# Attention pairs among the projections: values, scores and turns in one group instead of two

## The chip, the cores and the metric

One core of one Trainium2 chip runs the whole kernel. The metric is the device time of one execution in microseconds; the median of three runs of the kernel before is 2280.51 us (2280.38 to 2281.26). Five engines work side by side and meet only at semaphores: PE (TensorE, matrix multiplies), DVE (VectorE), ACT (ScalarE), POOL (GpSimd) and SP (which here issues DMAs). Each runs its own instructions in the order in which they are written. A `wait_ge` stops everything behind it on that engine.

## The reference, cut to what matters

A trunk of two layers over 512 tokens of width 1024, in float32. Each layer is a gated feed-forward net, a token mixing of three branches, and a second feed-forward net. The change touches the first branch, attention, and the projections that run beside it:

```
z = h @ w_in[i]                       # h: 512 x 1024, one combined projection
q, k, v = z[..., 0:768], z[..., 768:1536], z[..., 1536:2304]   # 3 groups x 4 heads x 64
y_a = dilated_attention_mixture(q, k, v)
gates = sigmoid(z[..., G_OFF:] + b_gate[i])
merged = gates[0] * (y_a @ w_proj_a) + gates[1] * (y_b @ w_proj_b) + gates[2] * (y_c @ w_proj_c)
# attention of one group: s = q k^T / 8, masked to a dilated causal window;
# p = exp(s - max); o = (p @ v) / sum(p); the groups are mixed by their softmax denominators
```

## The kernel before, in words

Activations are kept transposed: channels on the 128 partitions, the 512 tokens along the free axis. Each float32 product is made of three passes over rounded parts (high x high, high x low, low x high), so a projection of 128 output channels is 8 x 3 = 24 matmuls of 512 columns, called a half here. A unit of weights is 1024 x 256, two halves. SP loads it into one of two raw buffers, ACT copies it rounded (`split` on ACT, L985), and DVE makes the rest (`split` on DVE, L1465). Then TensorE may use it, and the raw buffer is free for SP's next load.

The attention is worked in eight pairs (two heads, one residue of the token index modulo 4) per layer. The three dilation groups are one softmax over 640 keys, since mixing by denominators is the same as one common denominator. A pair needs:

- scores (`score_pair`, L869 and L877): matmuls in 64 x 64 tiles of the array, into `side[0]` for one head and `psum[1]` for the other, columns 0 to 639;
- on DVE the masked row maximum of each head (`score_max`, L2001) into `p_tile`, on ACT the exponential with its sum (`exponential`, L1367), on DVE the division (`normalise`, L2024 and L2025);
- turns (`turn_pair`, L889 and L894): five transposes of 128 columns for each head, the first head's into `side[1]`, the second's into `side[0]`, columns 0 to 639;
- on ACT the copies of the turned tiles into `pT` (`take_turned`, L1372 and L1374);
- values (`value_pair`, L909): 24 matmuls of 64 wide tiles into `side[1]`, columns 640 to 767;
- the head's output, copied rounded by ACT (`head_hi`, L1353), with the rest by DVE (`head_lo`, L1994), which then raises `head_made`.

All this stands between projection matmuls. `project_to(end)` (L852) issues projection matmuls up to number `end` of the 288 of the phase (twelve halves, for the remaining queries and keys and the first gates), all into `psum[0]`, whose two column halves alternate. A half may begin only when DVE has taken the half before the last (`take_half`, L1971, L1975, L2043, which raises `evacuated[0]`). Two lists written out by hand, `SCORES_AT` and `TURNS_AT`, say before which projection matmul each pair's work comes. At `SCORES_AT[n]` the scores of pair n are issued and behind them the values of pair n - 1; at `TURNS_AT[n]` the turns of pair n. So the projections are interrupted sixteen times in a layer; the values of the last pair follow the phase.

ACT and DVE have loops over the same eight pairs, with weight splits, halves and, on ACT for pairs 5 and 6, the gates' sigmoids (`sigmoids`, L1360) put in at fixed places. Sigmoid and exponential need different tables on ACT, and a table load stands at each switch. In ACT's loop the order for pair n is: head of pair n - 1, a split for n = 1 and 5, two exponentials, a split for n = 2, 3 and 6, the two copies of the turned tiles, the sigmoids.

`side` and `psum` tensors are 1024 columns wide, two banks of 512 columns each.

Of the kernel before, what the change touches and what calls it, by code (L numbers as in the profile page):

```python
# [23 lines left out]
ACT = mybir.ActivationFunctionType  # L24

P = 128
# [49 lines left out]
def trunk(nc, x, ffn1_norm, ffn1_w_gate, ffn1_w_up, ffn1_w_down, mix_norm, w_in, b_gate, b_ln_g,  # L76
# [16 lines left out]
    ATT = HEADS * RES  # L93
    PAIRS = ATT // 2
# [4 lines left out]
    KEYS = NEAR + 2 * P  # L99
# [23 lines left out]
    with ExitStack() as ctx:  # L123
# [196 lines left out]


        PHASE = 6 * 2 * 3 * KD
        SCORES_AT = (10, 48, 86, 124, 162, 194, 226, 258)
        TURNS_AT = (38, 76, 114, 152, 185, 217, 249, 281)
        MASK_STEPS = 1 + P // RES + (RES - 1) + 6 * RES


# [219 lines left out]
        def _(pe):  # L547
# [10 lines left out]
            def begin_side(s):  # L558
                pe.wait_ge(side_evacuated[s], counts[f"sv{s}"].next())
                return side[s]  # L560
# [179 lines left out]
            for layer in range(DEPTH):  # L740
# [100 lines left out]
                def project_to(end):  # L841

                    for q in range(stream["at"], end):
                        h, k, n = q // (3 * KD), q // 3 % KD, q % 3
                        c = h % 2
                        if q % (3 * KD) == 0:
                            pe.wait_ge(evacuated[0], free + max(h - 1, 0))
                            if c == 0:
                                stream["w"] = unit()
                        whi, wlo = stream["w"]  # L850
                        l, r = ((whi, h_hi), (whi, h_lo), (wlo, h_hi))[n]
                        mm = nc.tensor.matmul(psum[0][:, c * S:(c + 1) * S], l[:, k * UNIT_N + c * P:k * UNIT_N + (c + 1) * P],  # L852
                                              r[:, k * S:(k + 1) * S], start=(k == 0 and n == 0), stop=(k == KD - 1 and n == 2))
                        if k == KD - 1 and n == 2:
                            mm.then_inc(half_done if c == 0 else unit_done, 1)
                    stream["at"] = end
# [26 lines left out]
                def turn_pair(n):  # L883
                    pe.wait_ge(p_made, counts["p"].next())
                    if n == 0:

                        pe.wait_ge(side_evacuated[1], counts["sv1"].now(1))
                    for c in range(KEYS // P):
                        mm = nc.tensor.transpose(side[1][:, c * P:(c + 1) * P], p_tile[0][:, c * P:(c + 1) * P], ident[:, :])  # L889
                    mm.then_inc(pT_written, 1)  # L890
                    pe.wait_ge(p_made, counts["p"].next())
                    o = begin_side(0)
                    for c in range(KEYS // P):
                        mm = nc.tensor.transpose(o[:, c * P:(c + 1) * P], p_tile[1][:, c * P:(c + 1) * P], ident[:, :])  # L894
                    mm.then_inc(pT_written, 1)

                def value_pair(n):
                    jp, r = divmod(n, RES)

                    pe.wait_ge(pT_made, counts["pT"].next())  # L900
                    pe.wait_ge(side_evacuated[0], counts["sv0"].now(1 if n == PAIRS - 1 else 0))
                    pe.wait_ge(head_made, counts["head"].next())

                    parts = ((0, 1, P, 0, P), (0, 2, 2 * P, 0, P), (0, 0, 0, 0, HQ), (0, 3, HQ, HQ, P),
                             (1, r, NEAR, 0, P), (2, r, NEAR + P, 0, P))
                    for m, (g, t, c0, q0, q1) in enumerate(parts):
                        for b in range(2):
                            col = t * A_WIDTH + g * A_OUT + (2 * jp + b) * HEAD_DIM
                            mm = nc.tensor.matmul(side[1][rows_of(b), KEYS + q0:KEYS + q1], v[:, col:col + HEAD_DIM],  # L909
                                                  pT[b][:, c0:c0 + q1 - q0], start=(m == 0), stop=(m == len(parts) - 1))  # L910
                            if m == len(parts) - 1:
                                mm.then_inc(head_done, 1)

                for n in range(PAIRS):
                    project_to(SCORES_AT[n])
                    score_pair(n)
                    if n > 0:
                        value_pair(n - 1)
                    project_to(TURNS_AT[n])
                    turn_pair(n)  # L920
                project_to(PHASE)
                value_pair(PAIRS - 1)

                def project(last_head=False):
                    columns(begin(1), unit(), yb_hi, yb_lo, range(KB), True, True).then_inc(unit_done, 1)
# [46 lines left out]
        def _(act):  # L972
# [68 lines left out]
            def step(k=UNIT_K, n=UNIT_N, parts=1, home=None, before=0):  # L1041

                split(k, n, parts, home, before)
                counts["unit"].next()
# [201 lines left out]
            for layer in range(DEPTH):  # L1246
# [96 lines left out]
                counts["ev1"].next()  # L1343

                counts["sd0"].next(PAIRS)
                counts["se0"].next(ATT)
                counts["sd1"].next()

                def head_hi(n):
                    jp, r = divmod(n, RES)  # L1350
                    act.wait_ge(head_done, counts["head"].next(2))
                    dst = ya_hi[:, jp * S:(jp + 1) * S].rearrange("p (i r) -> p r i", r=RES)[:, r, :]
                    nc.scalar.activation(dst, side[1][:, KEYS:KEYS + P], ACT.Copy).then_inc(ya_hi_made, 1)  # L1353
# [14 lines left out]
                                         accum_out=row_sum[:, b:b + 1]).then_inc(exp_made, 1)  # L1368

                def take_turned():  # L1370
                    act.wait_ge(pT_written, counts["pT_written"].next())
                    nc.scalar.activation(pT[0][:, :], side[1][:, 0:KEYS], ACT.Copy).then_inc(pT_made, 1)  # L1372
                    act.wait_ge(pT_written, counts["pT_written"].next())
                    nc.scalar.activation(pT[1][:, :], side[0][:, 0:KEYS], ACT.Copy).then_inc(side_evacuated[0], 1)  # L1374

                bias_col = T_BGATE + layer * (3 * KD)
                counts["ev0"].next(6)
# [1 line left out]
                for n in range(PAIRS):  # L1379
                    if n == 0:  # L1380
                        step(parts=2)
                    if n > 0:
                        head_hi(n - 1)
                    if n == 1:
                        step(parts=2)
                    if n == 5:
                        step()
                    for b in range(2):
                        exponential(b)
                    if n in (2, 3):  # L1390
                        step()
                    if n == 6:
                        step(KB)
                    take_turned()
                    if n in (5, 6):

                        counts["ev0"].next()
                        sigmoids(n - 5, 0, bias_col)
                head_hi(PAIRS - 1)
                counts["ev0"].next()  # L1400

# [39 lines left out]
        def _(dve):  # L1441
            counts = {k: Count() for k in ("unit", "hi", "step", "h_hi", "sq", "acc", "side0", "side1", "std", "rstd",
                                           "silu", "act_hi", "gelu", "ln_std", "yc_hi", "yb_hi", "exp",
                                           "head", "gate", "merged", "pooled", "y", "half", "scored_b", "unit7",
                                           "l0", "l1", "l2", "s_hi", "t", "acc_hi", "pool_hi")}
            counts |= {k: Count(1) for k in ("ev0", "ev1", "se0", "se1")}
            slot = [0]

# [377 lines left out]
            for layer in range(DEPTH):  # L1826
# [181 lines left out]

                def score_max(n):
                    dve.wait_ge(side_done[0], counts["side0"].next())  # L2010
                    nc.vector.memset(small[:, 126:127], 0.0)
                    v_ = side_out(0, masked_max(n, 0, side[0]))
                    dve.wait_ge(side_evacuated[0], v_)
                    negate(0)
                    counts["se0"].next()
                    dve.wait_ge(scored_b, counts["scored_b"].next())
                    nc.vector.memset(small[:, 126:127], 0.0)
                    v_ = evac(1, masked_max(n, 1, psum[1]))
                    dve.wait_ge(evacuated[1], v_)
                    negate(1)  # L2020
# [23 lines left out]
                                                        rstd[:, :], ALU.mult))  # L2044

                for n in range(PAIRS):
                    score_max(n)
                    if n > 0:
                        head_lo(n - 1)
                    normalise(0)  # L2050
                    normalise(1)
                    if n < 4:
                        take_half((0, 2, 3, 5)[n])
                        split()
                        if n in (0, 2):
                            take_half((1, None, 4)[n])
                    elif n in (4, 7):
                        take_half(6 if n == 4 else 10)
                        take_half(7 if n == 4 else 11)
                    elif n == 5:  # L2060
                        split()
                        take_half(8)
                    else:
                        take_half(9)
                        split(KB)
                head_lo(PAIRS - 1)

                def project(d):
# [69 lines left out]
```

## Time and profile before

| | us |
|---|---|
| median of 3 runs | 2280.51 |
| the profiled execution | 2280.67 |
| its span | 2278.9 |
| TensorE busy | 2269.5 (100%) |
| DVE busy | 1535.8 (67%) |
| ACT busy | 854.7 (38%) |
| POOL busy | 31.0 (1%) |
| DMA, mean over the span | 98 GB/s |

The granted clock of TensorE is at full speed (2.4 GHz) in all 40 slices of the span. Busy time of TensorE is that of pipelined matmuls, whose ends overlap the starts of the next, so the time from start to start tells more than the length. The phase of the change lies at 499.6 to 596.0 us in the first layer and at 1627.2 to 1723.6 us in the second. The profiled execution took 1.8 us more than its span, and 0.16 us more than the median.

### The profile page before, as it was taken

The page shows a single profiled execution, that of the slowest core. Times are in us where ns is not written, and L with a number is a line of the kernel's source. Part 1 is how long each engine was busy: PE and PEld are TensorE (multiplying, and loading weights), DVE is VectorE, ACT ScalarE, POOL GpSimd, SP SyncE. Part 2 cuts the span into 40 slices and gives each one's busy share as a digit, 9 for nine tenths or more (in the row PEclk, how much of TensorE's full clock was granted, in tenths as well). Part 3 has the DMA queues.
Part 4 walks back from the last instruction along what each step waited for, and adds up shares of the span by engine and source line. Part 5 has one row for each costly group of instructions (what it writes and reads, how often), then busy time and mean ns, then how long its engine had stood idle before and what let it go on. Part 6 is the DMA issues. An engine that isn't in the chain of part 4 may idle for free.

```text
span 2278.9 us, 31164 instructions
## 1 busy us (share of the span) xinstructions
PE 2269.5 (100%) x13365; PEld 1988.8 (87%) x13365; DVE 1535.8 (67%) x1728; ACT 854.7 (38%) x936; POOL 31.0 (1%) x70
## 2 busy tenths in 40 slices
PE   9999999999999999999999999999999999999998
PEld 8898998888888888989888989888888888899897
DVE  6895977545543668959568959675554455698694
ACT  5443433323522334424334424342344224344342
POOL 5000000000000000000000000000000000000000
PEclk9999999999999999999999999999999999999999
DMA  5324233321223332323323333342212332233231
GB/s 163 97 93 129 75 111 116 93 78 61 79 83 100 117 97 88 112 93 112 103 89 104 99 106 97 107 134 65 83 52 83 102 115 94 79 109 128 76 114 70
DMA packets 231393, 222.66 MB, mean 98 GB/s; under 512 B 4209, under 2 KB 229601, under 8 KB 231265
## 3 DMA queue, kind: packets, MB, share of 16 engines
q1 hardware_dynamic: 225744, 215.29, 29.9%
q10 hardware_dynamic: 5520, 5.51, 0.7%
q8 instruction: 99, 1.62, 0.3%
q14 instruction: 30, 0.24, 0.0%
HBM read 218.69 MB, written 2.10 MB: 97 GB/s over the span
## 4 chain that ended last, share of the span: by engine, by line
PE 100%; DVE 0%; POOL 0%; DVEq 0%; issue 0%; ACT 0%; POOLq 0%
PE psum L584 56%; PE psum L632 16%; PE side L632 12%; PE psum L852 6%; PE psum L786 2%; PE side L584 1%; PE psum L596 1%; PE side L909 1%; PE side L869 1%; PE psum L734 0%; PE side L889 0%; PE side L894 0%; PE side L797 0%; PE side L877 0%; PE side L766 0%; PE psum L708 0%
## 5 line engine op out<-in xcount | busy, mean ns | idle before, releaser
L584 PE MATMUL psum<-h_hi,w_hi 128*128 128x512 f32 x928 | 361.9, 390 | 0.0
L584 PE MATMUL psum<-h_hi,w_lo 128*128 128x512 f32 x928 | 361.1, 389 | 0.0
L584 PE MATMUL psum<-h_lo,w_hi 128*128 128x512 f32 x928 | 361.0, 389 | 0.0
L1465 DVE TENSOR_TENSOR w_lo<-raw,w_hi 128x2048 fp32r<-128x2048 f32 (+2 forms) x123 | 239.2, 1945 | 80.7 <-ACT w_hi L985 80.0
L632 PE MATMUL psum<-s_hi,hi 128*128 128x256 f32 x1024 | 289.8, 283 | 0.0
L632 PE MATMUL psum<-s_lo,hi 128*128 128x256 f32 x1024 | 289.8, 283 | 0.0
L985 ACT ACTIVATE w_hi<-raw 128x2048 fp32r<-128x2048 f32 (+2 forms) x123 | 200.9, 1633 | 228.9 <-PE psum L584 198.7
L584 PE MATMUL psum<-act_hi,w_lo 128*128 128x512 f32 x704 | 273.9, 389 | 0.0
L1094 ACT ACTIVATE hi<-t_sum 128x1536 fp32r<-128x1536 f32 (+1 forms) x128 | 134.2, 1055 | 264.7 <-DVE t_sum L1660 264.7
L584 PE MATMUL psum<-act_hi,w_hi 128*128 128x512 f32 x576 | 224.1, 389 | 0.0
L584 PE MATMUL psum<-act_lo,w_hi 128*128 128x512 f32 x576 | 224.1, 389 | 0.0
L632 PE MATMUL psum<-s_hi,t_lo 128*128 128x256 f32 x768 | 217.3, 283 | 0.0
L632 PE MATMUL side<-s_lo,hi 128*128 128x256 f32 x768 | 217.3, 283 | 0.0
L632 PE MATMUL side<-s_hi,hi 128*128 128x256 f32 x768 | 217.3, 283 | 0.0
L584 PEld LDWEIGHTS psum<-h_hi,w_lo 128*128 128x128 f32 x928 | 174.2, 188 | 36.3
L584 PEld LDWEIGHTS psum<-h_hi,w_hi 128*128 128x128 f32 x928 | 174.2, 188 | 36.0
L584 PEld LDWEIGHTS psum<-h_lo,w_hi 128*128 128x128 f32 x928 | 174.2, 188 | 35.9
L632 PEld LDWEIGHTS psum<-s_hi,hi 128*128 128x128 f32 x1024 | 196.6, 192 | 0.0
L632 PEld LDWEIGHTS psum<-s_lo,hi 128*128 128x128 f32 x1024 | 196.6, 192 | 0.0
L1532 DVE SCALAR_TENSOR_TENSOR xT<-psum,xT 128x1024 f32<-128x1024 f32 x53 | 64.8, 1224 | 139.6 <-PE psum L584 139.3
L584 PEld LDWEIGHTS psum<-act_hi,w_lo 128*128 128x128 f32 x704 | 132.1, 188 | 27.4
L632 PEld LDWEIGHTS side<-s_hi,hi 128*128 128x128 f32 x768 | 147.4, 192 | 0.3
(285 smaller groups left out, 4318.0 us busy)
## 6 DMA issues: line engine op xcount, KB each, us to landing
raw<-in_ffn_w_up_dram SPq DMA_DIRECT2D x44, 1024.0 KB, 5.4
raw<-in_ffn_w_gate_dram SPq DMA_DIRECT2D x43, 1024.0 KB, 5.4
raw<-in_w_in_dram SPq DMA_DIRECT2D x42, 1024.0 KB, 5.3
raw<-in_ffn_w_down_dram SPq DMA_DIRECT2D x32, 1024.0 KB, 5.0
raw<-in_ffn_w_down_dram SPq DMA_DIRECT2D x16, 768.0 KB, 4.4
raw<-in_w_in_dram SPq DMA_DIRECT2D x24, 512.0 KB, 4.1
raw<-in_w_out_dram SPq DMA_DIRECT2D x8, 1024.0 KB, 5.0
raw<-in_w_proj_b_dram SPq DMA_DIRECT2D x8, 512.0 KB, 3.4
```

The source lines that it names most:

```text
L584: mm = nc.tensor.matmul(dst[:, c * S:(c + 1) * S], l[:, a], r[:, b], start=first and k == ks[0] and n == 0, stop=last and k == ks[-1] and ...
L596: mm = nc.tensor.matmul(o, l[:, k * P:(k + 1) * P], r[:, k * S:(k + 1) * S], start=(k == 0 and n == 0), stop=(k == KD - 1 and n == 2))
L632: mm = nc.tensor.matmul(o[:, col:col + HALF], l(k), r[:, b], start=k == 0 and n == 0, stop=k == KH - 1 and n == 2)
L786: mm = nc.tensor.matmul(d, l[:, k * S + t * P:k * S + (t + 1) * P], w[:, part, k], start=(k == 0 and m == 0), stop=(k == KD - 1 and m == 2))
L852: mm = nc.tensor.matmul(psum[0][:, c * S:(c + 1) * S], l[:, k * UNIT_N + c * P:k * UNIT_N + (c + 1) * P], r[:, k * S:(k + 1) * S], start=( ...
L869: nc.tensor.matmul(outs[b][h * HQ:(h + 1) * HQ, col:col + k1 - k0], t[rows_of(b), q + h * HQ:q + (h + 1) * HQ], t[rows_of(b), k + k0:k + k ...
L909: mm = nc.tensor.matmul(side[1][rows_of(b), KEYS + q0:KEYS + q1], v[:, col:col + HEAD_DIM], pT[b][:, c0:c0 + q1 - q0], start=(m == 0), sto ...
L985: nc.scalar.activation((home[0] if home else w_hi[s])[:, 0:k * n], raw[s][:, 0:k * n], ACT.Copy).then_inc(hi_made, 1)
L1094: nc.scalar.activation(dst, src, ACT.Copy).then_inc(hi_made, 1)
L1465: nc.vector.tensor_tensor(lo[:, a], raw[s][:, a], hi[:, a].bitcast(F32), ALU.subtract).then_inc(split_made, 1)
L1532: i_ = nc.vector.scalar_tensor_tensor(x_, src, scale, x_, ALU.mult, ALU.add)
```

## The change

TensorE interrupts the projections at the places of one list. Group n holds the values of pair n - 2, the scores of pair n and the turns of pair n - 1, in this order. Groups 0 to 8 stand among the projections (0: scores alone; 1: scores and turns; 8: values and turns), the last values behind them as before. The second head's turned tiles move to columns 640 and up: three of them in `side[0]`, two in `psum[1]`; ACT copies them in two pieces, ahead of the first head's. TensorE's turns wait, from pair 1 on, for `head_made` of the values in the same group. DVE's maximum of pair n waits for the copies of the second head's turned tiles of pair n - 1. On ACT and DVE each head is worked one pair later, and ACT's copies of the turned tiles come ahead of the exponentials. In the diff TensorE's part comes first, then ACT's (from `take_turned`), then DVE's (from `score_max`).

```diff
-        SCORES_AT = (10, 48, 86, 124, 162, 194, 226, 258)
-        TURNS_AT = (38, 76, 114, 152, 185, 217, 249, 281)
+        GROUPS_AT = (10, 48, 82, 122, 162, 194, 220, 245, 270, PHASE)
+        TURNED_B = KEYS
...
                     mm.then_inc(pT_written, 1)
                     pe.wait_ge(p_made, counts["p"].next())
-                    o = begin_side(0)
                     for c in range(KEYS // P):
-                        mm = nc.tensor.transpose(o[:, c * P:(c + 1) * P], p_tile[1][:, c * P:(c + 1) * P], ident[:, :])
+                        o, at_ = (side[0], TURNED_B + c * P) if c < 3 else (psum[1], TURNED_B + (c - 3) * P)
+                        mm = nc.tensor.transpose(o[:, at_:at_ + P], p_tile[1][:, c * P:(c + 1) * P], ident[:, :])
                     mm.then_inc(pT_written, 1)
 
                 def value_pair(n):
...
-                    pe.wait_ge(pT_made, counts["pT"].next())
-                    pe.wait_ge(side_evacuated[0], counts["sv0"].now(1 if n == PAIRS - 1 else 0))
+                    pe.wait_ge(pT_made, counts["pT"].next(2))
                     pe.wait_ge(head_made, counts["head"].next())
...
-                for n in range(PAIRS):
-                    project_to(SCORES_AT[n])
-                    score_pair(n)
-                    if n > 0:
-                        value_pair(n - 1)
-                    project_to(TURNS_AT[n])
-                    turn_pair(n)
-                project_to(PHASE)
-                value_pair(PAIRS - 1)
+                for n in range(PAIRS + 2):
+                    project_to(GROUPS_AT[n])
+                    if n > 1:
+                        value_pair(n - 2)
+                    if n < PAIRS:
+                        score_pair(n)
+                    if 0 < n <= PAIRS:
+                        if n > 1:
+                            pe.wait_ge(head_made, counts["head"].now(1))
+                        turn_pair(n - 1)
...
                 def take_turned():
-                    act.wait_ge(pT_written, counts["pT_written"].next())
+                    act.wait_ge(pT_written, counts["pT_written"].next(2))
+                    nc.scalar.activation(pT[1][:, 0:3 * P], side[0][:, TURNED_B:TURNED_B + 3 * P], ACT.Copy)
+                    nc.scalar.activation(pT[1][:, 3 * P:KEYS], psum[1][:, TURNED_B:TURNED_B + 2 * P], ACT.Copy).then_inc(pT_made, 1)
                     nc.scalar.activation(pT[0][:, :], side[1][:, 0:KEYS], ACT.Copy).then_inc(pT_made, 1)
-                    act.wait_ge(pT_written, counts["pT_written"].next())
-                    nc.scalar.activation(pT[1][:, :], side[0][:, 0:KEYS], ACT.Copy).then_inc(side_evacuated[0], 1)
...
                 for n in range(PAIRS):
                     if n == 0:
                         step(parts=2)
+                    if n > 1:
+                        head_hi(n - 2)
                     if n > 0:
-                        head_hi(n - 1)
+                        take_turned()
                     if n == 1:
                         step(parts=2)
...
                     if n == 6:
                         step(KB)
-                    take_turned()
                     if n in (5, 6):
...
+                head_hi(PAIRS - 2)
+                take_turned()
                 head_hi(PAIRS - 1)
...
                 def score_max(n):
                     dve.wait_ge(side_done[0], counts["side0"].next())
+                    if n > 0:
+                        dve.wait_ge(pT_made, counts["pT"].next(2) - 1)
...
                 for n in range(PAIRS):
+                    if n > 1:
+                        head_lo(n - 2)
                     score_max(n)
-                    if n > 0:
-                        head_lo(n - 1)
                     normalise(0)
                     normalise(1)
...
-                    elif n in (4, 7):
-                        take_half(6 if n == 4 else 10)
-                        take_half(7 if n == 4 else 11)
+                    elif n == 4:
+                        take_half(6)
+                        take_half(7)
+                    elif n == 7:
+                        take_half(10)
...
+                counts["pT"].next(2)
+                head_lo(PAIRS - 2)
+                take_half(11)
                 head_lo(PAIRS - 1)
```

## Rows read from the trace of the kernel before

**Rows 1.** The page, part 1: engine, busy us (share), instructions.

```profile
PE 2269.5 (100%) x13365; PEld 1988.8 (87%) x13365; DVE 1535.8 (67%) x1728; ACT 854.7 (38%) x936; POOL 31.0 (1%) x70
```

**Rows 2.** The page, part 4: the chain that ended last, by engine.

```profile
PE 100%; DVE 0%; POOL 0%; DVEq 0%; issue 0%; ACT 0%; POOLq 0%
```

**Rows 3.** Busy time of each engine in the first layer's phase.

```profile
499.55:595.95 96.40, 96.40 (x786) 78.30 (x784) 51.74 (x122) 45.55 (x70) 0.00 (x0) 1.00 0.19 58
```

**Rows 4.** The chain of waits in order of time: start, length, what.

```profile
488.83 10.88 PE psum L596 x48
```

**Rows 5.** Timeline, TensorE, pairs 0 and 1: start, length, engine, line, operation.

```profile
501.59 0.39 PE L852 MATMUL psum<-h_hi,w_hi 128*128 128x512 f32 x1
...
509.45 0.39 PE L852 MATMUL psum<-h_lo,w_hi 128*128 128x512 f32 x1
509.69 0.71 PE L889 MATMUL side<-ident,p_tile 128*128 128x128 f32 x5
510.23 0.71 PE L894 MATMUL side<-ident,p_tile 128*128 128x128 f32 x5
510.69 0.48 PE L852 MATMUL psum<-h_hi,w_lo 128*128 128x512 f32 x1
511.01 0.39 PE L852 MATMUL psum<-h_hi,w_hi 128*128 128x512 f32 x1
...
512.85 0.39 PE L852 MATMUL psum<-h_hi,w_lo 128*128 128x512 f32 x1
513.16 0.53 PE L869 MATMUL side<-qk 64*64 64x384 f32 x1
...
514.41 1.33 PE L909 MATMUL side<-pT,v 128*64 128x128 f32 x24
515.67 0.50 PE L852 MATMUL psum<-h_hi,w_hi 128*128 128x512 f32 x1
...
521.93 0.40 PE L852 MATMUL psum<-h_hi,w_hi 128*128 128x512 f32 x1
```

**Rows 6.** Timeline at the phase's end, TensorE, ACT and DVE.

```profile
594.37 0.40 PE L852 MATMUL psum<-h_hi,w_lo 128*128 128x512 f32 x1
594.69 1.33 PE L909 MATMUL side<-pT,v 128*64 128x128 f32 x24
...
596.09 0.41 ACT L1353 ACTIVATE ya_hi<-side 128x128 fp32r<-128x128 f32 x1 [2.16 <-PE side L909]
...
596.53 0.40 DVE L1994 TENSOR_TENSOR ya_lo<-side,ya_hi 128x128 fp32r<-128x128 f32 x1 [1.04 <-ACT ya_hi L1353]
```

**Rows 7.** Forms of L852 and L909: count, then ns min/median/max.

```profile
L852 PE MATMUL psum<-h_lo,w_hi x192: 387/389/504, 499.8 to 1721.8; 128*128 128x512 f32 x192
...
L909 PE MATMUL side<-pT,v x384: 219/272/323, 514.4 to 1723.4; 128*64 128x128 f32 x128, 128*64 128x64 f32 x64
```

**Rows 8.** Timeline, ACT, pairs 5 and 6.

```profile
564.61 1.93 ACT L985 ACTIVATE w_hi<-raw 128x2048 fp32r<-128x2048 f32 x1
566.43 0.81 ACT L1367 ACTIVATE p_tile<-p_tile,small 128x640 f32<-128x640 f32 x1
...
571.69 1.28 ACT L1360 ACT_TABLE_LOAD   x1
572.99 1.33 ACT L1360 ACTIVATE gate<-gate,table 128x512 f32<-128x512 f32 x2
...
578.97 1.06 ACT L985 ACTIVATE w_hi<-raw 128x1024 fp32r<-128x1024 f32 x1
```

**Rows 9.** Timeline, DVE, pair 5.

```profile
568.85 2.29 DVE L1465 TENSOR_TENSOR w_lo<-raw,w_hi 128x2048 fp32r<-128x2048 f32 x1
571.05 0.69 DVE L2043 TENSOR_TENSOR gate<-psum,rstd 128x512 f32<-128x512 f32 x1
```

**Rows 10.** ACT's copies out of PSUM of 256 and 640 columns: ns min/median/max.

```profile
L1154 ACT ACTIVATE wide<-side x64: 361/366/370, 112.3 to 2215.5; 128x256 f32<-128x256 f32 x64
...
L1372 ACT ACTIVATE pT<-side x16: 706/706/710, 510.4 to 1720.3; 128x640 f32<-128x640 f32 x16
```

More of the change, by code:

```diff
@@ L1345, in _ @@
                 counts["sd0"].next(PAIRS)
-                counts["se0"].next(ATT)
+                counts["se0"].next(PAIRS)
                 counts["sd1"].next()
@@ L1444, in _ @@
                                            "head", "gate", "merged", "pooled", "y", "half", "scored_b", "unit7",
-                                           "l0", "l1", "l2", "s_hi", "t", "acc_hi", "pool_hi")}
+                                           "l0", "l1", "l2", "s_hi", "t", "acc_hi", "pool_hi", "pT")}
             counts |= {k: Count(1) for k in ("ev0", "ev1", "se0", "se1")}
@@ L2014, in score_max @@
                     negate(0)
-                    counts["se0"].next()
                     dve.wait_ge(scored_b, counts["scored_b"].next())
```

## The prediction

> **What bounds the kernel now.** I read the busy shares first, then the chain of waits, then the phase that the change touches, instruction by instruction. TensorE is busy for 2269.5 of 2278.9 us [rows 1], and the chain that ended last is TensorE's to 100% [rows 2]. So a change counts only by what it does to the order, the length and the gaps of TensorE's own stream. The phase (projection matmuls of L852 with the attention pairs between them) is 96.40 us of each layer at a granted clock of 1.00 [rows 3]. A run of matmuls of 512 columns goes at 10.88 / 48 = 0.2267 us each, start to start [rows 4]. The phase has 288 of them, 65.28 us; what stands between them is 31.1 us. No stretch of TensorE in it waits for another engine; its gaps are those at a change from one kind of matmul to another.
>
> **What an interruption costs now.** From the last projection matmul before it to one some steps later, less 0.2267 a step [rows 5]:
> - turns (ten transposes): 509.45 to 512.85, ten steps: 3.40 - 2.27 = 1.13 us. The transposes run at 0.54 / 5 = 0.109 us each, so 1.09 us is the work. An interruption by turns alone costs almost nothing beyond it.
> - scores alone: 501.59 to 509.45, 28 steps: 7.86 - 6.35 = 1.51.
> - scores and values: 512.85 to 521.93, 28 steps: 9.08 - 6.35 = 2.73.
> - values alone, behind the phase, up to the next matmul: 1.26 + 0.32 [rows 6].
>
> **The change on TensorE, with no wait.** Each old pair has 1.13 + 2.73 = 3.86. The new group is values, scores, turns, and I add it from blocks: entry into the values 0.32 (594.37 to 594.69 [rows 6]; about the same into the scores, 512.85 to 513.16 [rows 5]); values to next block 1.26 (514.41 to 515.67); scores to next block 1.25 (513.16 to 514.41); turns to the second matmul behind them 1.32 (509.69 to 511.01); the steps behind it are 0.03 longer in sum (511.01 to 512.85, eight steps) [rows 5]. Not shown before is a transpose that directly follows 64-wide tiles. A first projection matmul there is 504 instead of 389 ns and a first value matmul 323 instead of 272 [rows 7] (+0.115 and +0.05). The transpose (272 ns) is nearer to the value matmul in length, so I take 0.07 for it, with 0 and 0.115 as bounds. Sum 4.25, less two steps (0.45): 3.80. Six such groups save 6 x 0.06 = 0.36. The group of scores 1 and turns 0 is 0.32 + 1.25 + 1.32 + 0.10 - 0.45 = 2.54 against 2.64: saves 0.10. The group of values 6 and turns 7 is 2.55, against 2.73 - 1.51 = 1.22 for the values within the old group plus 1.13: costs 0.20. The first scores and the last values stay. Nothing is won by "one interruption for two": 0.36 + 0.10 - 0.20 = 0.26, or 0.36 if I total the phase (31.1 measured, against 1.51 + 2.54 + 22.80 + 2.55 + 1.36 = 30.76). I take 0.36 us per layer. Bounds: if the turns' first step is 0.115 dearer, 0.0; if it costs nothing, and the 0.20 gap from scores to the next block shrinks to the 0.10 between values (both halves), 1.7.
>
> The rows say why: of the old 16 breaks the eight turn breaks had no price. The Trainium skill (TensorEngine Tiling (Array Packing), Key Properties) says that a change of tiling mode drains the TensorE. By that rule turns, which use the whole array as the projections do, were free to enter and leave, and the new group has the same three changes (projection to values, to scores, to turns) as the old score group; the trace agrees, 0.24 us from projection to transpose against 0.31 from projection to scores. By that rule alone the saving would be 0 where the rows give 0.36.
>
> **What the change adds: waits on the head.** From pair 1 on, the turns wait for head_made of the values in the same group. These values have to be copied by ACT (L1353) and subtracted by DVE (L1994) first. Queued behind that wait on TensorE are the ten transposes and all projections. The clean chain is at the end of the phase [rows 6]: values 594.69 + 1.33 = 596.02, ACT 596.09 to 596.50, DVE 596.53 to 596.93: 0.91 us. For DVE to TensorE no row shows a hop; I take 0.05, like the 0.03 and 0.07 of the other two. So the turns may start 0.96 behind the end of the values.
> - Groups 2 to 5: the scores stand between. Turns would start 1.26 + 1.25 - 1.33 = 1.18 behind that end: covered with 0.22 to spare, if both engines are free. Counting on from each group's end, they are (DVE's last split ends about 0.6 us or more before the copy of the head does, the tightest being group 2).
> - Group 8 (values 6, turns 7): no scores between. The turns would start 0.07 before the values end, so TensorE waits 0.96 + 0.07 = 1.03 us. This is certain by the order alone; bounds 0.96 and 1.15.
> - Group 6: let E be the end of the turns of group 5. 26 matmuls, then values and scores: the second matmul is at E + 0.07, the 26th 5.47 later, turns due at 5.54 + 0.32 + 1.26 + 1.25 = E + 8.37. ACT copies the three parts of the turned tiles first (about 0.47, 0.37 and 0.71, overlapped by 0.1) [rows 10], to E + 1.38, then the weight split (starts E + 1.28; exponentials 1.82 later [rows 8]), then DVE's chain: 2.42 from the first exponential to its own split, that 2.29 and overlapped, gate half 8 up to 2.89 behind the split's start [rows 8, 9]. E + 1.28 + 1.82 + 2.42 + 2.89 = 8.41, head 0.30 net, hop 0.05: E + 8.76. TensorE waits 0.39. ACT's sigmoids end at about E + 7.5 and aren't last. Bounds 0 and 0.8.
> - Group 7: turns due at E + 8.14 (25 matmuls). ACT's split for the next phase needs half 9, whose last matmul ends at E + 4.57: split 4.67 to 5.74 (1.06), table load 1.28, two sigmoids 1.33 [rows 8]: E + 8.39. Only then the head's copy (0.3 net), DVE 0.42, hop: E + 9.16. TensorE waits 1.02. The sigmoids used to stand behind the turns' copies, where nothing waited; now they stand in front of the head. Bounds 0.6 and 1.4.
>
> Together 0.39 + 1.02 + 1.03 = 2.44 us per layer.
>
> **What else moves, at nothing.** DVE's row maxima now wait for the copies of the turned tiles (E + 0.8) in place of following the scores; behind them are queued exponentials, normalisations, halves and splits. Probabilities are then ready at E + 4.5 (5.6 with an ACT split before, 5.3 with a table load) and are wanted at 8.1 or later. Halves: the tightest is half 6, taken by about E + 5.2, wanted at E + 6.7. Weight splits are three us or more early, and so the DMAs of SP's queue, issued when a split frees its raw buffer, move by a us or two with a whole unit (over 10 us) of cover. The copy in three in place of two costs ACT 0.1. If the cover of a half or split were gone, each us late would be a us on TensorE.
>
> **Sum.** 2.44 - 0.36 = 2.08 per layer, 4.2 for two. The profiled execution has 2280.67, 0.16 over the median 2280.51: so 2284.7 (+0.18%). About 0.2% (4.6 us) is what a measurement can tell from no change, so this lies just inside.
>
> **Rivals.**
> - Slower: the scores don't cover the head in groups 2 to 5. It decides from 1.18 us between the end of the values and the release of TensorE. If that takes 1.40, four groups pay 0.22 and the other three 0.44 more each: +2.2 per layer, 2289.1. For: the slack is 0.22 and the last hop is on no row. Against: all hops shown are 0.03 to 0.07. Chance 0.12.
> - Slower: a switch of ACT's table stops it for twice the 1.28 us of the load. Then the wait of group 6 is 1.15 (by ACT, not DVE) and that of group 7 3.3: 1.15 + 3.3 + 1.03 - 0.36 = 5.1 per layer, 2290.7. Against: the sigmoid begins 0.02 behind the load's end [rows 8]. Chance 0.03. The Trainium skill (ScalarE: Activation LUTs, What ACT_TABLE_LOAD costs) gives a drain of about 1380 ns besides the load of 1283, by which the time would be near 2291; this trace has the load and not the drain.
> - Only group 8 waits, since ACT and DVE run ahead of my count: 1.03 - 0.36 = 0.67 per layer, 2281.8. For: two long chains added from rows. Chance 0.14.
> - Faster: breaks are dearer than counted (saving 1.7) and only group 8 waits: -1.4 to -3, 2279 or so. Against: turns alone cost 1.13 for 1.09 of work. Chance 0.05, and hardly ever beyond 0.2%.
>
> **How the numbers follow.** The forecast has 0.66, own range 2283.4 to 2285.9, and 0.20 of it lies above 2285.07. Slower by over 0.2%: 0.20 + 0.12 + 0.03 = 0.35; faster 0.03; within 0.62. The range 2281.4 to 2286.6 leaves out most of the slower rivals and the faster one.
>
> **What would show it.** Profile after: transposes of group 8 start about 1.0 us later than the values end, released by DVE's L1994-line; group 7 the same, behind sigmoids; group 6 by a few tenths, behind DVE's gate half; groups 2 to 5 without a gap; phase 98.5 us in place of 96.4; a transpose behind scores at a first step of about 0.18. It is wrong if groups 2 to 5 show gaps, if group 7 has none, or if the phase without its waits is shorter by over 1 us.

## The result, and the profile after

The changed kernel takes 2284.44 us, the median of 20 runs (2284.08 to 2285.28), against 2280.82 (20 runs, 2280.29 to 2281.52) for the kernel before on the same chips. The ratio is 1.0016, 95% interval 1.0010 to 1.0023: 3.6 us slower, 0.16%. The forecast was 2284.7, range 2281.4 to 2286.6, with the higher chance on a difference within 0.2%. In the comparisons below, two executions of the kernel before ran at a lower granted clock (0.85 and 0.556; 2480.51 and 3784.57 us) and are left out of the ratios.

The page after, parts 1 and 4, which answer to [rows 1] and [rows 2]:

```profile
PE 2268.5 (99%) x13365; PEld 1988.5 (87%) x13365; DVE 1537.8 (67%) x1728; ACT 857.1 (38%) x952; POOL 30.2 (1%) x70
...
PE 98%; ACT 1%; DVE 1%; DMA 0%; issue 0%; DVEq 0%; ACTq 0%
```

TensorE's busy time fell by 1.0 us, and the span rose. ACT and DVE now hold 1% each of a chain that was TensorE's alone: the new time is waits, not work.

The phase in both layers, busy time by engine (columns as in [rows 3]):

```profile
499.26:597.53 98.27, 96.11 (x785) 78.23 (x784) 52.57 (x122) 46.98 (x78) 0.00 (x0) 1.00 0.19 57
1628.84:1727.12 98.28, 96.12 (x785) 78.23 (x784) 52.60 (x122) 46.98 (x78) 0.00 (x0) 1.00 0.19 57
```

The phase is 1.87 and 1.88 us longer than the 96.40 of [rows 3], at the same granted clock. The two together are 3.75, and the medians differ by 3.6. Outside the phases only the time before the first one differs, by 0.29 (499.26 against 499.55); among the profiles of the experiments it lies between 499.26 and 499.76, in kernels that are alike up to there, so this is scatter between executions.

The timeline of the kernel after, TensorE, ACT and DVE, around groups 2, 6, 7 and 8 (start, length, engine, line, operation, and in brackets the idle time before it with what ended it):

```profile
521.67 0.39 PE L852 MATMUL psum<-h_hi,w_hi 128*128 128x512 f32 x1
521.99 1.33 PE L908 MATMUL side<-pT,v 128*64 128x128 f32 x24
523.25 0.53 PE L869 MATMUL side<-qk 64*64 64x384 f32 x1
...
524.50 0.77 PE L889 MATMUL side<-ident,p_tile 128*128 128x128 f32 x5
...
525.56 0.48 PE L852 MATMUL psum<-h_lo,w_hi 128*128 128x512 f32 x1
...
534.52 0.39 PE L852 MATMUL psum<-h_lo,w_hi 128*128 128x512 f32 x1
...
568.04 2.28 DVE L1468 TENSOR_TENSOR w_lo<-raw,w_hi 128x2048 fp32r<-128x2048 f32 x1
568.39 1.33 PE L908 MATMUL side<-pT,v 128*64 128x128 f32 x24
...
569.90 0.40 ACT L1353 ACTIVATE ya_hi<-side 128x128 fp32r<-128x128 f32 x1
570.25 0.68 DVE L2047 TENSOR_TENSOR gate<-psum,rstd 128x512 f32<-128x512 f32 x1
570.85 0.37 DVE L1997 TENSOR_TENSOR ya_lo<-side,ya_hi 128x128 fp32r<-128x128 f32 x1
571.27 0.77 PE L889 MATMUL side<-ident,p_tile 128*128 128x128 f32 x5 [0.31 <-DVE ya_lo L1997]
...
577.25 1.06 ACT L985 ACTIVATE w_hi<-raw 128x1024 fp32r<-128x1024 f32 x1 [0.22 <-PE psum L852]
...
578.22 1.33 PE L908 MATMUL side<-pT,v 128*64 128x128 f32 x24
578.33 1.28 ACT L1360 ACT_TABLE_LOAD   x1
579.63 1.33 ACT L1360 ACTIVATE gate<-gate,table 128x512 f32<-128x512 f32 x2
580.87 0.37 ACT L1353 ACTIVATE ya_hi<-side 128x128 fp32r<-128x128 f32 x1
581.27 0.38 DVE L1997 TENSOR_TENSOR ya_lo<-side,ya_hi 128x128 fp32r<-128x128 f32 x1 [1.70 <-ACT ya_hi L1353]
581.71 0.77 PE L889 MATMUL side<-ident,p_tile 128*128 128x128 f32 x5 [0.91 <-DVE ya_lo L1997]
...
588.65 1.33 PE L908 MATMUL side<-pT,v 128*64 128x128 f32 x24
...
590.05 0.39 ACT L1353 ACTIVATE ya_hi<-side 128x128 fp32r<-128x128 f32 x1 [2.58 <-PE side L908]
590.48 0.38 DVE L1997 TENSOR_TENSOR ya_lo<-side,ya_hi 128x128 fp32r<-128x128 f32 x1 [1.63 <-ACT ya_hi L1353]
590.91 0.77 PE L889 MATMUL side<-ident,p_tile 128*128 128x128 f32 x5 [0.94 <-DVE ya_lo L1997]
```

How to read it. In group 2 the transposes (L889) start 1.25 behind the scores, the time that the scores took before the values in the kernel before (513.16 to 514.41 [rows 5]): no wait. That no bracket stands there would not show it by itself, since a wait of 0.2 us can go without one (see the doubled low part below). In groups 6, 7 and 8 a bracket stands, and the releaser is each time DVE's low part of the head (L1997). In group 8 the head's chain is alone: the values end at 588.65 + 1.33 = 589.98, the transposes start at 590.91, 0.93 later. In group 7 ACT is in a table load and two sigmoids when the values end (579.55), and the head's copy starts at 580.87 only. In group 6 ACT does its copy with a small delay, and DVE is still in the gate half (570.25 + 0.68 = 570.93) when the copy ends at 570.30. The bracket is somewhat less than the added time, since it is counted from modelled ends. So below a wait is the start-to-start distance from the last scores or values to the first transpose, less the 0.20 that it takes without a wait.

### The profile page after: what moved, and what is told of

Read it like the earlier page. It is cut to its first block, busy times and chain, and to the rows that moved or that the text cites. A ratio compares the mean times of both kernels' runs of the same rounds, so it can differ in the third digit from the quotient of the medians.

```text
span 2282.4 us, 31192 instructions
## 1 busy us (share of the span) xinstructions
PE 2268.5 (99%) x13365; PEld 1988.5 (87%) x13365; DVE 1537.8 (67%) x1728; ACT 857.1 (38%) x952; POOL 30.2 (1%) x70
## 4 chain that ended last, share of the span: by engine, by line
PE 98%; ACT 1%; DVE 1%; DMA 0%; issue 0%; DVEq 0%; ACTq 0%
PE psum L584 56%; PE psum L632 16%; PE side L632 12%; PE psum L852 5%; PE psum L786 2%; PE side L584 1%; PE psum L596 1%; PE side L908 1%; PE side L889 1%; PE psum L734 0%; PE side L869 0%; PE side L797 0%; DMA x_in<-in_x_dram 0%; ACT w_hi L985 0%; PE side L766 0%; PE side L808 0%
```

## Experiments

The phase's length is given for the first layer; the second differs by 0.02 us or less. Each of the first four was compared with the kernel before at 2280.88 (33 runs), the last four at 2280.68 (29 runs), on one chip each. "Less than after" is a difference to 2284.44, which was measured with another set; the medians of the kernel before differ by 0.2 us between the sets.

**Turns before the values in group 8.** TensorE turns pair 7 before the values of pair 6, so that it needs only the head of pair 5:

```
+    if n == PAIRS:                       # TensorE
+        pe.wait_ge(head_made, counts["head"].now(1))
+        pe.wait_ge(pT_made, counts["pT"].now(2))
+        turn_pair(n - 1)
...
+    act.wait_ge(head_made, (layer + 1) * PAIRS)   # ACT, before its last copies
```

> In group 8 alone the turns of pair 7 are issued ahead of the values of pair 6, so that they wait for no head of their own group; ACT's copy of those turned tiles waits until the head of pair 6 is done. Theory (three waits of TensorE for a head: 0.38, 0.98 and 1.01 us in groups 6, 7 and 8 of each layer): the 1.01 goes, and going from transposes to values and from values to projections costs about 0.17 more than before, so -0.84 per layer: -1.7 against the changed kernel, +1.9 against the kernel before. Rival (the wait only moves on, to the last values, whose tiles are now copied later): no change against the changed kernel, +3.6 against the kernel before.

Measured: 2282.59 (11 runs, 2282.18 to 2283.21), ratio 1.0007 [0.9998, 1.0016]; 1.85 less than after. The timeline of this kernel, TensorE, group 8:

```profile
588.43 0.40 PE L852 MATMUL psum<-h_hi,w_lo 128*128 128x512 f32 x1
588.66 0.71 PE L889 MATMUL side<-ident,p_tile 128*128 128x128 f32 x5
589.21 0.49 PE L894 MATMUL side<-ident,p_tile 128*128 128x128 f32 x3
...
589.85 1.33 PE L908 MATMUL side<-pT,v 128*64 128x128 f32 x24
591.10 0.50 PE L852 MATMUL psum<-h_hi,w_hi 128*128 128x512 f32 x1
...
595.09 0.39 PE L852 MATMUL psum<-h_hi,w_lo 128*128 128x512 f32 x1
```

The transposes of group 8 start 0.23 behind the projection, as in the kernel before, the waits of groups 6 and 7 stay (0.38 and 0.99), and the phase is 97.32, 0.95 less. The wait has not moved on to the last values, which start 0.32 behind the last projection (595.09 to 595.41). So this wait is the order's alone, and half of the loss is this one place. The phase gives back 0.06 less than the 1.01 of the wait: group 8 by itself costs 595.09 - 588.43 = 6.66, less 18 steps (4.08), 2.58; after, it was 2.53 without its wait (588.33 to 595.95: 7.62 - 4.08 - 1.01). So the new order costs 0.05 to 0.06 and not the 0.17 expected.

**Both sigmoids behind the last pair.** ACT's work alone is moved:

```
-    if n in (5, 6):
-        counts["ev0"].next()
-        sigmoids(n - 5, 0, bias_col)
...
+for g in range(2):                       # behind the loop over the pairs
+    counts["ev0"].next()
+    sigmoids(g, 0, bias_col)
```

> ACT works the sigmoids of the first two gates together behind the exponentials of pair 7, not behind those of pairs 5 and 6; two of the phase's table loads to and fro go. Theory (group 7 waits since the head's copy is queued on ACT behind a table load and two sigmoids): the 0.98 of group 7 goes, the 0.38 of group 6 stays (there DVE's gate half is last) and the 1.01 of group 8 stays: -2.0 against the changed kernel, +1.6 against the kernel before. Rival A (ACT's table switches are not on the path, group 7 waits for DVE's split): no change. Rival B (group 6 hangs on ACT too): -2.7.

Measured: 2283.59 (11 runs, 2283.32 to 2284.27), ratio 1.0012 [1.0003, 1.0021]; only 0.85 less than after, where 2.0 was expected. Four table loads per layer go, not two (ACT has 944 instructions in place of 952). Group 7's wait is gone, as expected, and group 6's is the same 0.38. But group 8's grew from 1.01 to 1.63. The timeline of this kernel there, ACT, DVE and TensorE:

```profile
586.20 1.28 ACT L1360 ACT_TABLE_LOAD   x1
587.50 2.56 ACT L1360 ACTIVATE gate<-gate,table 128x512 f32<-128x512 f32 x4
587.91 1.33 PE L908 MATMUL side<-pT,v 128*64 128x128 f32 x24
...
589.96 0.37 ACT L1353 ACTIVATE ya_hi<-side 128x128 fp32r<-128x128 f32 x1
...
590.80 0.77 PE L889 MATMUL side<-ident,p_tile 128*128 128x128 f32 x5 [1.56 <-DVE ya_lo L1996]
```

The values end at 589.24. The four sigmoids, now in one run, end at 590.06, and the head's copy starts with their last 0.1 us. I had expected them done by then; I had moved them from one head's path into the next one's. It confirms the mechanism of group 7 (sigmoids in front of the head's copy), by removing it there and by making it again elsewhere. 0.98 - 0.62 = 0.36 per layer, and the phase is 97.92, 0.35 less.

**Gate half 8 behind the head.** DVE's order alone:

```
+    if n == 6:                           # behind head_lo(n - 2)
+        take_half(8)
...
-        take_half(8)                     # in the branch of n == 5
```

> DVE takes gate half 8 behind the head of pair 4, not ahead of it. Theory (group 6 waits since DVE has a weight split and then this half in front of the head): the wait of group 6 falls from 0.38 to under 0.05 us, -0.7 against the changed kernel, +2.9 against the kernel before. Rival (group 6 waits for ACT, whose sigmoids end just then): no change, +3.6. Second rival (half 8 taken later stops half 10): a gap in the projections at matmul 240, slower than the changed kernel.

Measured: 2283.87 (11 runs, 2283.35 to 2284.44), ratio 1.0013 [1.0004, 1.0022]; 0.57 less than after, and the phase 97.89, 0.38 less. The timeline of this kernel, group 6:

```profile
568.89 1.33 PE L908 MATMUL side<-pT,v 128*64 128x128 f32 x24
...
570.40 0.40 ACT L1353 ACTIVATE ya_hi<-side 128x128 fp32r<-128x128 f32 x1
...
570.83 0.42 DVE L1997 TENSOR_TENSOR ya_lo<-side,ya_hi 128x128 fp32r<-128x128 f32 x1
571.13 0.68 DVE L2047 TENSOR_TENSOR gate<-psum,rstd 128x512 f32<-128x512 f32 x1
571.40 0.77 PE L889 MATMUL side<-ident,p_tile 128*128 128x128 f32 x5
```

The half (L2047) stands behind the head, and the transposes start 2.51 behind the values (568.89 to 571.40), as in group 2 (521.99 to 524.50): no wait. Groups 7 and 8 wait as before this edit, and nothing waits for half 8, which is now taken later. It was the gate half, not ACT, that was last in group 6.

**All three together.** The three edits above in one kernel.

> The three edits together: group 8 with turns first, the sigmoids late, half 8 behind the head. Theory: none of the three waits is left and what remains is what merging gives: 2.2 us less per layer than the changed kernel, -4.4, that is -0.8 against the kernel before (2280.0). Rival (a part of the 1.9 us per layer that the phase grew by is not these waits but dearer breaks): the phase stays over 96.4 us and the time at or above that of the kernel before.

Measured: 2280.05 (11 runs, 2279.42 to 2280.29), ratio 0.9996 [0.9987, 1.0005]. With the sigmoids late and the turns of group 8 ahead of the values, no head is waited for. The phase of this kernel:

```profile
499.26:595.23 95.97, 95.97 (x786) 78.37 (x784) 52.71 (x122) 43.51 (x75) 0.00 (x0) 1.00 0.20 59
```

The median is where the theory had it (2280.0), though the interval holds 1: it is the phase that shows the gain. It is busy in all of its length, 0.43 less than [rows 3] and 2.30 less than after. This is the change without its waits: what the merged interruptions are worth is 0.4 us per layer, 0.8 us in all, less than a single wait of 1 us in both layers costs. Group 8, with turns first, costs 2.60 here (586.97 to 593.65: 6.68 - 4.08).

**The head's low part made twice.** DVE computes it twice and releases TensorE by the second, which makes the head's chain about 0.4 us longer:

```
+    chain(low_part())
+    low_part().then_inc(head_made, 1)
```

> The changed kernel with DVE's low part of each head computed twice, one behind the other, before head_made is raised: 0.42 us more between the values and the release of TensorE. Theory (released 0.93 us behind the end of the values, as group 8 shows, and due at 1.18 in groups 2 to 5, so 0.25 to spare): gaps of 0.17 us appear in groups 2 to 5, and those of groups 6, 7 and 8 grow by 0.42 each; 1.96 per layer, +3.9 against the changed kernel, +7.5 against the kernel before. Rival (in groups 2 to 5 the scores cover far more than that): only the three waits grow, +2.5 and +6.1.

Measured: 2288.66 (6 runs, 2288.33 to 2289.38), ratio 1.0036 [1.0023, 1.0048]; 4.2 more than after, where 3.9 was expected. The timeline of this kernel, group 2:

```profile
523.69 0.41 ACT L1353 ACTIVATE ya_hi<-side 128x128 fp32r<-128x128 f32 x1 [4.28 <-PE side L908]
524.13 0.82 DVE L1998 TENSOR_TENSOR ya_lo<-side,ya_hi 128x128 fp32r<-128x128 f32 x2 [0.79 <-ACT ya_hi L1353]
...
525.01 0.77 PE L889 MATMUL side<-ident,p_tile 128*128 128x128 f32 x5
```

Groups 6, 7 and 8 wait 0.42 longer each, and groups 2 to 5, which waited for nothing, wait 0.21 each. These four carry no bracket; the wait is read from the start, 2.72 behind the values in place of 2.51 (522.29 to 525.01). So their cover was 0.42 - 0.21 = 0.21 us (0.22 in the prediction). I had expected 0.25, from the 0.93 of group 8; but in group 2 of the kernel after the head's chain is 0.97 (the values end at 523.32, the low part at 523.83 + 0.40, and the hop is 0.06 as from 524.95 to 525.01 here), since copy and low part are 0.02 longer each than in group 8. It shows how near the kernel stood to the slower rival: one more 0.2 us on the head and every group pays. Phase 100.36: 3 x 0.42 + 4 x 0.21 = 2.10 against 2.09 measured.

**Eight more breaks by transposes.** The kernel before, with the second five transposes of each pair four projections later than the first:

```
+    project_to(TURNS_AT[n] + 4)          # between the two heads' transposes
```

> The kernel before, with the ten transposes of each pair in two interruptions, four projection matmuls apart: eight more interruptions per layer, by full-array transposes. Theory (a break to transposes and back costs only some slow steps, 0.04 us): +0.6 for both layers. Rival (any interruption costs the 0.24 us by which scores alone and values alone exceed both in one): +3.8.

Measured: 2281.29 (12 runs, 2280.78 to 2281.89), ratio 1.0003 [0.9994, 1.0011], +0.6. The phase is 96.63, 0.23 over [rows 3]. The timeline of this kernel at the phase's end, ACT and TensorE:

```profile
594.21 0.70 ACT L1375 ACTIVATE pT<-side 128x640 f32<-128x640 f32 x1 [0.76 <-PE side L895]
594.48 0.40 PE L852 MATMUL psum<-h_hi,w_lo 128*128 128x512 f32 x1
595.01 1.33 PE L910 MATMUL side<-pT,v 128*64 128x128 f32 x24
```

0.21 of the 0.23 is here: the last values start 0.53 behind the projection in place of 0.32 [rows 6], because ACT's copy of the later transposes ends at 594.91. From the first projection to the last, the phase takes 594.48 - 499.64 = 94.84 in place of 94.82 (499.55 to 594.37). So all eight added breaks cost about 0.02 us, and one under 0.01. The theory had +0.6 as well, but by 0.04 for each break: the time agrees by luck, since most of it is the wait at the end.

**Values apart from the scores.** The kernel before, with two projections between scores and values in seven pairs:

```
+    project_to(SCORES_AT[n] + 2)         # before value_pair
```

> The kernel before, with two projection matmuls between the scores and the values of each pair from 1 on: seven more interruptions per layer, by 64-wide tiles. Theory (what costs is going into and out of such tiles): 0.24 us each, +3.4 for both layers. Rival (an interruption as such is free and what matters is the work): under +0.6. A wait for the probabilities of pair 5 would show as a gap before its transposes.

Measured: 2283.97 (12 runs, 2283.35 to 2284.34), ratio 1.0015 [1.0006, 1.0024], +3.3. The phase of this kernel:

```profile
499.51:597.43 97.92, 97.92 (x785) 77.80 (x784) 52.39 (x122) 45.42 (x70) 0.00 (x0) 1.00 0.19 57
```

Busy throughout, 1.52 longer: 0.22 us for each of seven breaks by 64-wide tiles. Beside the kernel above this separates the two kinds: a break by full-array transposes costs almost nothing, one more by tiles of half the array 0.22 (into them and out of them again).

**Values 6 and 7 in one run.** From the experiments: the three edits, and since a break by 64-wide tiles is what costs, the values of pair 6 go to the end beside those of pair 7. Pair 7's turned tiles and values have buffers of their own, so neither pair waits for the other, and ACT's wait for the head of pair 6 goes. DVE takes half 11 ahead of both heads:

```
     if n == PAIRS:                       # TensorE, as with turns before values
         pe.wait_ge(head_made, counts["head"].now(1))
         pe.wait_ge(pT_made, counts["pT"].now(2))
         turn_pair(n - 1)
+        continue
...
+        if n > PAIRS:
+            pe.wait_ge(pT_made, counts["pT"].now(4))
+            value_pair(PAIRS - 2)
         value_pair(n - 2)                # for pair 7 from pT_last into side[0]
...
+                take_turned(pT_last)     # ACT, ahead of the head of pair 6
```

> The changed kernel without head waits (sigmoids late, half 8 behind the head) in which group 8 is the turns of pair 7 alone, and the values of pairs 6 and 7 follow one another behind the phase; the turned tiles of pair 7 go to another place in SBUF and its values to side[0], so that neither waits for the head of pair 6. Theory (turns alone cost 1.13; second values behind the first 1.06 and a step of 0.10, so 2.3 for what takes 2.6 with turns first and a break of its own): -0.3 per layer against e4_no_head_wait, 2279.4, -1.4 against the kernel before. Rival (the heads of both pairs pile up on ACT and DVE behind the phase, and the next projections wait): at or above 2280.0.

Measured: 2278.89 (12 runs, 2278.78 to 2279.68), ratio 0.9993 [0.9984, 1.0002]. Its median is 5.5 us below after and 1.8 below the kernel before; all its runs are below the lowest of that kernel (2280.21), but the interval holds 1. The phase of this kernel:

```profile
499.31:594.90 95.59, 95.59 (x786) 78.34 (x784) 52.70 (x122) 43.39 (x75) 0.00 (x0) 1.00 0.20 59
```

0.38 less than with the three edits (0.3 expected), and 0.81 less than [rows 3], or 1.6 us for two layers.

## Why the prediction was right

Predicted 4.2 us more, measured 3.6 by the medians. The waits were right one by one, and the saving, the smaller term, was set too small (0.36 of 0.50); both misses go the same way, so the sum did not come out by errors that cancel. Per layer, in us:

| Step | predicted | measured | shown by |
|---|---|---|---|
| wait of group 6 | 0.39 | 0.38 | trace; gone when the half goes behind the head |
| wait of group 7 | 1.02 | 0.98 | trace; gone when the sigmoids go behind the loop |
| wait of group 8 | 1.03 | 1.01 | trace; gone when the turns go ahead |
| groups 2 to 5 | 0, 0.22 to spare | 0, 0.21 to spare | doubled low part |
| merged breaks | -0.36 | -0.50 | trace; -0.43 in the kernel with the three edits |
| phase | +2.08 | +1.88 | windows |

- **The waits** hold to 0.04 us. The term that no row before had shown, the hop from DVE to TensorE, was taken as 0.05 and is 0.05 (590.48 + 0.38 to 590.91); the whole chain, from 588.65 + 1.33 to 590.91, is 0.93 in group 8, where 0.96 was forecast, and 0.97 in group 2. Group 6 was the longest sum of durations and is right to 0.01; the gate half is what ended last in it, as forecast.
- **The saving** is the term that was off, by 0.14 per layer. A group of values, scores and turns costs 3.78 (521.67 to 534.52, 40 steps: 12.85 - 9.07), where 3.80 was added up; six of them make 0.12. The term that was mis-sized is the transpose behind 64-wide tiles, set at +0.07. The forms of L889 in the kernel after show it: count, then ns min/median/max.

```profile
L889 PE MATMUL side<-ident,p_tile x80: 272/273/329, 513.0 to 1721.0; 128*128 128x128 f32 x80
```

- The longest is 329 ns against 272, and the first step behind the scores is 0.164 against 0.109 (524.50 to 525.10 is 0.60 for five, less 4 x 0.109): +0.055 in place of +0.07. The rest of the 0.02 is in the blocks around. Scores with turns came to 2.53 (forecast 2.54), and values with turns to 2.53 (2.55).
- **Where the saving comes from.** "Nothing is won by one interruption for two" holds as said: a turn's break that is taken away is worth under 0.01 us (0.02 / 8), and the 64-wide breaks are as many as before. Yet the phase without its waits is 0.4 to 0.5 shorter, which the prediction had in its sum (0.07 for a transpose behind 64-wide tiles, where it had 0.115 for a projection [rows 7]) without naming it as the cause. It is the way out of the 64-wide tiles. In the kernel before they are left into projections, and the 27 steps behind the values lose 0.14 (515.67 to 521.93 [rows 5]: 6.26 - 6.12). In the new groups they are left into transposes, which lose 0.055; what the projections lose behind transposes is 0.12 in both (510.69 to 512.85, nine steps: 2.16 - 2.04; 525.56 to 534.52, 39 steps: 8.96 - 8.84). That is about 0.09 for a group, and the groups as a whole say the same: 3.88 for an old pair (512.85 to 525.34 in the kernel before, 38 steps: 12.49 - 8.61) against 3.78. The turns put before the values show it the other way round: there the values of group 8 are left into projections again, and the group costs 0.05 more.
- **The rule on modes.** The Trainium skill (TensorEngine Tiling (Array Packing), Key Properties) says that a change of tiling mode drains the TensorE; the pair of kernels with added breaks agrees, 0.22 us where the mode changes and under 0.01 where it does not.
- **The rivals.** The slower one (scores don't cover the head) is out: 0.93 to 0.97 us, where it needed more than 1.18. The stop of ACT for a second 1.28 us is out: the sigmoids of group 7 start at 579.63, 0.02 behind the load's end (578.33 + 1.28), and the load 0.02 behind the end of the split ahead of it (577.25 + 1.06), against the drain of about 1380 ns that the Trainium skill gives (ScalarE: Activation LUTs, What ACT_TABLE_LOAD costs). That only group 8 waits is out, and so is the large saving: without waits it is 0.4 to 0.5 per layer, not 1.7.
- **What I missed** came later, in an expectation: moving both sigmoids behind the last pair lengthens another head's queue. The prediction had looked for what stands in front of each head on ACT; for my own edit I had not.

The saving in the kernel after (0.50, the phase less its waits) and in the kernel with the three edits (0.43) differ by 0.07 us. That is group 8: 2.53 with values first, its wait taken off, against 2.60 with turns first. Left open is only why a transpose behind 64-wide tiles is held up by less than a projection there; the runs show the two prices and no reason.

## What to carry to other kernels

Before merging interruptions of a TensorE stream, price each kind of break by itself, measured from the last instruction before it to one well behind it: here only those that change the tile's width cost anything (0.22 us), and the merge took away the other kind; its 0.09 us per group came from what now follows the 64-wide tiles. So price the exits too: which instruction stands behind such tiles. A step moved up next to its producer changes a covered latency into a wait, so for each such place compare the producer's chain over the other engines (0.93 to 0.97 us here) with the work between, and list what stands in front of that chain on each engine; a table load, two sigmoids or one gate half is enough. Where a wait appears, moving what is queued in front of it is the cheap repair, if the new place is not in front of the next one.

## What the runs showed of the hardware

- A break in the stream of 512-column matmuls by full-array transposes costs under 0.01 us (eight added: 0.02); one more by 64-wide tiles, between two such matmuls, 0.22 us (seven added: 1.52).
- A full-array transpose directly behind 64-wide tiles takes 329 ns in place of 272, and delays the stream by 0.055 us. Where projections follow the values instead, 27 of them lose 0.14 us against 0.2267 a step.
- From the end of value matmuls, over a 128-column copy on ACT and a subtraction on DVE, back to TensorE takes 0.93 us (group 8) to 0.97 (group 2); the hop from DVE to TensorE is 0.05 (590.48 + 0.38 to 590.91).
- A table load on ACT takes 1.28 us, begins 0.02 us behind the instruction ahead of it, and the sigmoid begins 0.02 us behind its end (group 7 of the kernel after).
